# High parts of the weight slabs beside the retention: from GpSimd to ScalarE

## The chip, the cores and the metric

The kernel runs on one core of one Trainium2 chip. The metric is the device time of one execution in microseconds (us). The engines are named as in the profile: PE is TensorE (matmuls, and transposes done as matmuls; PEld is its weight load), DVE is VectorE, ACT is ScalarE, POOL is GpSimd, SP is SyncE, which here issues the DMAs.

## The reference

The program is one layer of a streaming encoder on a sequence of 1024 tokens with 1024 features, all in float32. The part that matters here is the retention branch and the input projection that runs beside it:

```python
h = rmsnorm(x, ln_pre_mix[layer])
p = h @ w_in[layer]                       # one combined projection
(g_q, g_k, g_v, g_r, g_lr, r_q, r_k, r_v, r_g, a_gla, a_ret) = jnp.split(p, split_at, axis=-1)
...                                       # gated linear attention (GLA) branch
rq = rope(r_q.reshape(b, s, RET_HEADS, RET_DK), positions)
rk = rope(r_k.reshape(b, s, RET_HEADS, RET_DK), positions)
# retention_mixer, per chunk and head:
scores = jnp.einsum('bhnd,bhmd->bhnm', qi, ki) * intra_decay
o = jnp.einsum('bhnm,bhme->bhne', scores, vi) + jnp.einsum('bhnd,bhde->bhne', qi * q_decay, state)
state = chunk_decay * state + jnp.einsum('bhmd,bhme->bhde', ki * k_decay, vi)
# then
o_ret = head_layernorm(o_ret) * silu(r_g)
y_ret = o_ret @ w_ret_out[layer]
merged = sigmoid(a_gla) * y_gla + sigmoid(a_ret) * y_ret
...                                       # m @ W_o, norm, and the ConvFFN
```

`rope` is the rotary embedding: the first half of a head's features becomes x1·cos − x2·sin, the second x1·sin + x2·cos.

## The kernel before

**Products in three parts.** Each large float32 product is made of three fast matmuls: both operands are split into a high part (the value written in TensorE's fp32r format) and a low part (the value minus its high part), and `product3` (lines 421 to 423) adds high·high, low·high and high·low. So each slab of weights, 128 partitions by 1024 columns, is needed as `w_hi` and `w_lo`, made from the loaded `w_raw`. All three have four slots (`RING`), used in turn.

**How slabs move.** SP loads slab n into `w_raw` (`stream_load`, line 1355) once slab n−4 has been split (`slab_ready`). Somebody writes `w_hi` (this counts `hi_split` up), then somebody writes `w_lo` (this counts `slab_ready` up), and PE waits for `slab_ready` before it uses the slab (`side_piece`, line 1320). `w_hi` may be overwritten once PE has used slab n−4 (`mm_half`). In other stages of this program ScalarE writes `w_hi` with a copy of the same shape and GpSimd writes `w_lo` (lines 3109 and 3098, the down projection of the FFN, for one). Beside the GLA and the retention, GpSimd does both, in `split_slab` (line 1360).

**The retention.** It has 32 steps (`RS`), e = 0 to 31: token tile e // 4 (128 tokens) and head e % 4. Every engine runs its own list of instructions in a fixed order, one list per function (`ret_pe`, `ret_dve`, `ret_act`, `ret_pool`, `ret_sp`), and they meet only at semaphores. What one step holds, in order:

- PE, step e: wait for the rotated queries and keys of step e (`r_rope`), transposes of the keys (line 2058), scores (2067), for e < 28 a quarter of a projection slab (`side_piece`, 12 matmuls), the transposes of the output of step e−2 (2107), the output of step e−1 (2085 and, from the second token tile on, 2088), the input to the state of step e−1 (2098).
- DVE, step e: weights of step e (1985), gate of step e−2 (1994), the mean and variance of the output of step e−1 (2003, 2005), its normalisation (2010), the state (2019 or 2021).
- ACT, step e: a scaled copy of the transposed keys of step e (`keys`, 1949), the reciprocal deviation of step e−1 (`rstd`, 1956 and 1959, which wait for DVE's 2005), in odd steps the eviction of a side bank (1341).
- POOL, step e: the rotation of step e (1920, 1921, 1929, 1931) and the decayed queries (1934). 1929 waits until PE has made the output of step e−4. For e = 0, 4, ..., 24 a slab follows (`split_slab`: 1365 for `w_hi`, 1368 for `w_lo`), and one more after step 31.
- SP, step e: stores, loads of the inputs of step e+4 and, for e = 0, 4, ..., 28, the load of a slab.

The slab that POOL splits in step e is used by PE from step e+8 on (the slabs split in the steps 20 and 24 and after the loop belong to the next stage).

Of the kernel before, what the change touches and what calls it, by code (L numbers as in the profile page):

```python
# [19 lines left out]
F32 = mybir.dt.float32  # L20
F32R = mybir.dt.float32r
I32 = mybir.dt.int32
ALU = mybir.AluOpType
ACT = mybir.ActivationFunctionType
# [71 lines left out]
SL_SIDE = SL_VAL + 4 * N_PLAIN + 1  # L96
# [14 lines left out]
BLOCK_LOADS = ROW_LOADS + BLOCK_GROUPS  # L111
RING = 4
# [90 lines left out]
def build(nc, x, positions, w_stream, w_dec, b_dec, ln_post_mix, ln_post_ffn, ln_cols_in, conv_in,  # L203
          ident_in, interval_in, masks_in, ret_dec_in, ret_q_in, ret_k_in, inv_freq_in, eps_in, out):
    ctx = ExitStack()
    with ctx:
        sem = {name: ctx.enter_context(nc.semaphore(name)) for name in SEMS}
# [15 lines left out]
        def sb(stack, name, shape, dt=F32):  # L223
            return stack.enter_context(nc.sbuf_tensor(name, list(shape), dt))
# [12 lines left out]
        w_raw = sb(ctx, "w_raw", (P, RING, D))  # L237
        w_hi = sb(ctx, "w_hi", (P, RING, D), F32R)
        w_lo = sb(ctx, "w_lo", (P, RING, D), F32R)
# [165 lines left out]
        raw_in = [sem[f"raw_in{j}"] for j in range(RING)]  # L405
# [902 lines left out]
        def tile_cols(t):  # L1308
            return slice(t * P, t * P + P)
# [26 lines left out]
        def side_evict(act, q):  # L1336

            act.wait_ge(sem["mm_half"], 2 * SL_SIDE + q + 1)
            if q >= SIDE_SLOTS:
                act.wait_ge(side_stored[q % SIDE_SLOTS], 16 * (q // SIDE_SLOTS))  # L1340
            nc.scalar.activation(side_out[:, q % SIDE_SLOTS, :], psum[:, SIDE_BANK + q % 2, :], ACT.Copy
                                 ).then_inc(sem["side_evac"], 1)
# [17 lines left out]
        def split_slab(pool, n):  # L1360

            j = n % RING
            pool.wait_ge(raw_in[j], 16 * (n // RING + 1 + BLOCK_LOADS))
            pool.wait_ge(sem["mm_half"], 2 * n - 2 * RING + 2)
            nc.gpsimd.tensor_tensor(w_hi[:, j, :], w_raw[:, j, :],
                                    zero_col[:, :].to_broadcast((P, D)), ALU.add).then_inc(sem["hi_split"], 1)
            pool.wait_ge(sem["hi_split"], n + 1)
            nc.gpsimd.tensor_tensor(w_lo[:, j, :], w_raw[:, j, :], w_hi[:, j, :].bitcast(F32),
                                    ALU.subtract).then_inc(sem["slab_ready"], 1)


        def gla_gates(sp, t):

            if t:
                sp.wait_ge(sem["g_og"], 2 * t)
            sp.dma_start(g_gate[:, :, :], proj_d[ROW_GR:ROW_GR + GLA_KT, :, tile_cols(t)]
                         .rearrange("r p n -> p r n")).then_inc(sem["g_gate_in"], 16)
# [14 lines left out]
        def gla_first_loads(sp):  # L1392

            sp.dma_start(masks[:, :], masks_in).then_inc(sem["g_tab_in"], 16)
            sp.dma_start(e_t[:, 0, :], interval_in).then_inc(sem["g_tab_in"], 16)
            gla_log_a_load(sp, 0)
            for t in range(2):
                gla_tile_loads(sp, t)
            gla_gates(sp, 0)
# [413 lines left out]
        def last_tile(e):  # L1813
            return e >= RS - HEADS
# [94 lines left out]
        def ret_pool(pool):  # L1909
            pool.wait_ge(sem["r_tab_in"], 64)  # L1910
            pool.wait_ge(sem["g_S"], 2 * NT * HEADS)
            for e in range(RS):
                t, h, b = e // HEADS, e % HEADS, e % 2
                x4 = r_x[:, h, 0:4, :]
                pool.wait_ge(r_in[h], 16 * t + 16)
                cos = cossin[:, 0, tile_cols(t)].unsqueeze(1).to_broadcast((P, 4, P))
                sin = cossin[:, 1, tile_cols(t)].unsqueeze(1).to_broadcast((P, 4, P))
                if e >= 2:
                    pool.wait_ge(sem["r_rope"], 2 * e - 2)
                nc.gpsimd.tensor_tensor(r_xcb[:, b, :, :], x4, cos, ALU.mult).then_inc(sem["r_xc"], 1)  # L1920
                nc.gpsimd.tensor_tensor(r_xsb[:, b, :, :], x4, sin, ALU.mult).then_inc(sem["r_xs"], 1)
                pool.wait_ge(sem["r_xc"], e + 1)
                pool.wait_ge(sem["r_xs"], e + 1)
                if t:
                    pool.wait_ge(sem["r_o"], e - 3)
                xc = r_xcb[:, b, :, :].rearrange("p (a c) n -> p a c n", c=2)
                xs = r_xsb[:, b, :, :].rearrange("p (a c) n -> p a c n", c=2)
                qk = r_qk[:, h, :, :].rearrange("p (a c) n -> p a c n", c=2)
                nc.gpsimd.tensor_tensor(qk[:, :, 0, :], xc[:, :, 0, :], xs[:, :, 1, :], ALU.subtract
                                        ).then_inc(sem["r_rope"], 1)  # L1930
                nc.gpsimd.tensor_tensor(qk[:, :, 1, :], xs[:, :, 0, :], xc[:, :, 1, :], ALU.add
                                        ).then_inc(sem["r_rope"], 1)
                pool.wait_ge(sem["r_rope"], 2 * e + 2)
                nc.gpsimd.tensor_tensor(r_qdb[:, h, :, :], r_qk[:, h, 0:2, :],
                                        ret_q[:, h, :].unsqueeze(1).to_broadcast((P, 2, P)),
                                        ALU.mult).then_inc(sem["r_qd"], 1)
                if e % 4 == 0 and e < RS - HEADS:
                    split_slab(pool, SL_SIDE + 19 + e // 4)
            split_slab(pool, SL_SIDE + 26)

        def ret_act(act):
            act.wait_ge(sem["r_tab_in"], 64)
            act.wait_ge(sem["g_og"], 2 * NT)

            def keys(e):
                act.wait_ge(sem["r_kT"], e + 1)
                if e >= 2:
                    act.wait_ge(sem["r_u"], e - 1)
                nc.scalar.activation(r_kdt[:, e % 2, :], psum[:, KT_BANK, 0:RET_DK], ACT.Copy,
                                     scale=ret_k[:, e % HEADS:e % HEADS + 1]).then_inc(sem["r_kd"], 1)  # L1950

            def rstd(e):

                b = e % 2
                act.wait_ge(sem["r_mv"], e + 1)
                nc.scalar.activation(r_rsb[:, b, 0:1], r_mvb[:, b, 1:2], ACT.Ln, bias=eps_col[:, 0:1]
                                     ).then_inc(sem["r_lnv"], 1)
                act.wait_ge(sem["r_lnv"], e + 1)
                nc.scalar.activation(r_rsb[:, b, 1:2], r_rsb[:, b, 0:1], ACT.Exp, scale=-0.5
                                     ).then_inc(sem["r_rstd"], 1)  # L1960

            for e in range(RS):
                if not last_tile(e):
                    keys(e)
                if e:
                    rstd(e - 1)
                if e < SIDE_STEPS and e % 2:
                    side_evict(act, 4 * NT + 2 + e // 2)
                if e >= MIXED_STEP:
                    for i in range(4 * (e - MIXED_STEP), 4 * (e - MIXED_STEP) + 4):  # L1970
                        mixed_hi(act, i)
            rstd(RS - 1)
            for i in range(8, 16):
                mixed_hi(act, i)
# [186 lines left out]
        def mixed_hi(act, i):  # L2161

            act.wait_ge(a_in[i % RING], 16 * (i // RING) + 32 + 16 * NT + 16)
            if i == 0:
                act.wait_ge(sem["mm_half"], 2 * SL_YGLA)
            if i == 16:
                act.wait_ge(sem["r_og"], RS)
                for b in range(2):
                    act.wait_ge(r_ogst[b], 8 * RS)
            if i == 16 + RET_KT:  # L2170
                act.wait_ge(sem["mm_half"], 2 * SL_YRET)
            nc.scalar.activation(mixed_parts(i)[0], a_raw[:, i % RING, :], ACT.Copy).then_inc(sem["a_hi"], 1)
# [1237 lines left out]
        @block.gpsimd  # L3410
        def _(pool):
            nc.gpsimd.memset(zero_col[:, :], 0.0).then_inc(sem["zero_set"], 1)
            nc.gpsimd.memset(eps_col[:, :], EPS).then_inc(sem["zero_set"], 1)
            pool.wait_ge(sem["zero_set"], 2)
            split_slabs(pool, 0, SL_LR)
            rows_pool(pool)
            split_slabs(pool, SL_LR + RING, SL_SIDE + 3, BLOCK_LOADS)
            gla_pool(pool)
            ret_pool(pool)
            split_slabs(pool, SL_YGLA + 3, SL_MIX, BLOCK_LOADS)  # L3420
            mix_pool(pool)
            up_pool(pool)
            slabs_lo(pool, SL_DOWN + RING, N_USED - SL_DOWN - RING)
# [55 lines left out]
```

## Time and profile before

| | us |
|---|---|
| median of 3 runs | 2281.41 (2281.05 to 2281.82) |
| the profiled execution, its own time | 2281.12 |
| its span, first to last instruction | 2279.3 |
| PE busy | 2243.6 (98%) |
| POOL busy | 1538.8 (68%) |
| DVE busy | 1209.4 (53%) |
| ACT busy | 669.2 (29%) |

The span is what the trace shows; the execution's own time is 1.8 us longer. "Busy" counts an engine's own instructions. A wait is idle time of an engine, put down to the instruction that released it. Matmuls are pipelined: a 512-column matmul is shown with 0.39 us, but the next one starts about 0.23 us after it.

### The profile page before, as it was taken

The numbers are of one execution on the slowest core, as the hardware profiler recorded it, in microseconds if no ns is written. First come the engines' busy times: TensorE is split into PE (matmuls) and PEld (weight loads), VectorE is DVE, ScalarE is ACT, GpSimd is POOL, SyncE is SP. The second block draws the span as 40 slices with busy tenths as digits, with TensorE's granted clock in tenths as the row PEclk, the third lists the DMA queues.
The fourth block names the chain that finished last, engine by engine and source line by source line (L and its number), as shares of the span: only waits on it lengthen the run. The fifth ranks groups of instructions, "written<-read, shape, count | busy, mean of one in ns | idle before, by whom it ended". The sixth has DMA issues, their size and how long they took to land. (4 is left out here: it accounts for less than half of the span.)

```text
span 2279.3 us, 27552 instructions
## 1 busy us (share of the span) xinstructions
PE 2243.6 (98%) x10462; PEld 1829.5 (80%) x10462; DVE 1209.4 (53%) x1271; ACT 669.2 (29%) x1029; POOL 1538.8 (68%) x946
## 2 busy tenths in 40 slices
PE   8999999999999999999999999999899999999998
PEld 7888888899888888876665888878778888888887
DVE  6322222222728877854446434323867777776564
ACT  4323333221222222211113211114444444443422
POOL 5787777766446555578664468870999999964442
PEclk9999999999999999999999999999999999999999
DMA  4333333322362333265557556642222222246444
GB/s 178 102 111 111 111 111 111 111 93 96 124 229 88 110 111 121 85 214 168 162 165 213 194 204 216 223 171 108 78 74 84 84 83 84 93 160 209 143 140 152
DMA packets 174716, 309.06 MB, mean 136 GB/s; under 512 B 12224, under 2 KB 90304, under 8 KB 174592
## 3 DMA queue, kind: packets, MB, share of 16 engines
q1 hardware_dynamic: 174160, 306.27, 40.8%
q8 instruction: 81, 1.33, 0.2%
q10 hardware_dynamic: 432, 1.11, 0.1%
q14 instruction: 43, 0.35, 0.0%
HBM read 217.16 MB, written 90.18 MB: 135 GB/s over the span
## 5 line engine op out<-in xcount | busy, mean ns | idle before, releaser
L421 PE MATMUL psum<-act_hi,w_hi 128*128 128x512 f32 x1272 | 505.4, 397 | 5.0 <-DVE act_lo L2178 1.4
L423 PE MATMUL psum<-act_hi,w_lo 128*128 128x512 f32 x1272 | 496.7, 391 | 0.0
L422 PE MATMUL psum<-act_lo,w_hi 128*128 128x512 f32 x1272 | 495.4, 389 | 0.0
L421 PEld LDWEIGHTS psum<-act_hi,w_hi 128*128 128x128 f32 x1272 | 239.0, 188 | 54.8 <-issue 2.9
L423 PEld LDWEIGHTS psum<-act_hi,w_lo 128*128 128x128 f32 x1272 | 238.7, 188 | 51.5
L422 PEld LDWEIGHTS psum<-act_lo,w_hi 128*128 128x128 f32 x1272 | 239.2, 188 | 46.9
L455 POOL TENSOR_TENSOR w_hi<-w_raw,zero_col 128x1024 fp32r<-128x1024 f32 x53 | 109.0, 2057 | 165.4 <-PE psum L423 147.7
L3098 POOL TENSOR_TENSOR w_lo<-w_raw,w_hi 128x1024 fp32r<-128x1024 f32 x44 | 110.5, 2515 | 126.5 <-ACT w_hi L3109 126.5
L1530 POOL TENSOR_TENSOR k_lev<-e_t,g_x 128x896 f32<-128x896 f32 x32 | 96.3, 3010 | 127.6 <-ACT e_t L1477 92.4
L1062 POOL TENSOR_TENSOR w_lo<-w_raw,w_hi 128x512 fp32r<-128x512 f32 x80 | 105.1, 1314 | 64.9 <-ACT w_hi L1020 64.9
L2796 DVE TENSOR_TENSOR d_lob<-d_raw,d_hib 128x512 fp32r<-128x512 f32 x44 | 101.9, 2320 | 86.9 <-ACT d_hib L2790 86.9
L458 POOL TENSOR_TENSOR w_lo<-w_raw,w_hi 128x1024 fp32r<-128x1024 f32 x53 | 143.8, 2714 | 4.2
L421 PE MATMUL psum<-w_hi,act_hi 128*128 128x512 f32 (+1 forms) x384 | 139.7, 364 | 1.8 <-POOL w_lo L458 1.5
L422 PE MATMUL psum<-w_lo,act_hi 128*128 128x512 f32 (+1 forms) x384 | 139.3, 363 | 0.0
L423 PE MATMUL psum<-w_hi,act_lo 128*128 128x512 f32 (+1 forms) x384 | 139.2, 363 | 0.0
L421 PE MATMUL psum<-w_hi,d_hib 128*128 128x512 f32 x352 | 137.3, 390 | 1.4 <-DVE act_f L2835 0.7
L422 PE MATMUL psum<-w_lo,d_hib 128*128 128x512 f32 x352 | 137.0, 389 | 0.0
L423 PE MATMUL psum<-w_hi,d_lob 128*128 128x512 f32 x352 | 137.0, 389 | 0.0
L3056 POOL TENSOR_TENSOR w_lo<-w_raw,w_hi 128x512 fp32r<-128x512 f32 x80 | 126.3, 1588 | 2.9 <-ACT w_hi L3138 2.8
L421 PE MATMUL psum<-a_sums,w_hi 128*128 128x512 f32 x320 | 124.5, 389 | 0.0
L422 PE MATMUL psum<-a_sums,w_hi 128*128 128x512 f32 x320 | 124.5, 389 | 0.0
L423 PE MATMUL psum<-a_sums,w_lo 128*128 128x512 f32 x320 | 124.5, 389 | 0.0
(300 smaller groups left out, 4947.3 us busy)
## 6 DMA issues: line engine op xcount, KB each, us to landing
w_raw<-in_w_stream SPq DMA_DIRECT2D x225, 512.0 KB, 4.0
proj_scratch<-stage SPq DMA_DIRECT2D x40, 512.0 KB, 5.0
r_x<-proj_scratch SPq DMA_DIRECT2D x64, 256.0 KB, 3.2
value_scratch<-stage SPq DMA_DIRECT2D x24, 512.0 KB, 3.6
proj_scratch<-side_out SPq DMA_DIRECT2D x48, 256.0 KB, 3.0
d_raw<-ffn_scratch SPq DMA_DIRECT2D x44, 256.0 KB, 3.7
ffn_scratch<-u_lin_v SPq DMA_DIRECT2D x20, 512.0 KB, 5.8
r_v<-value_scratch SPq DMA_DIRECT2D x32, 256.0 KB, 2.7
```

The costliest lines, as they stand in the source:

```text
L421: nc.tensor.matmul(o, s_hi, m_hi, start=start, stop=False)
L422: nc.tensor.matmul(o, s_hi, m_lo, start=False, stop=False)
L423: return nc.tensor.matmul(o, s_lo, m_hi, start=False, stop=stop)
L455: nc.gpsimd.tensor_tensor(w_hi[:, j, :], w_raw[:, j, :], zero_col[:, :].to_broadcast((P, D)), ALU.add).then_inc(sem["hi_split"], 1)
L458: nc.gpsimd.tensor_tensor(w_lo[:, j, :], w_raw[:, j, :], w_hi[:, j, :].bitcast(F32), ALU.subtract).then_inc(sem["slab_ready"], 1)
L1062: nc.gpsimd.tensor_tensor(w_lo8[:, n % 8, :], row_block(p, i), w_hi8[:, n % 8, :].bitcast(F32), ALU.subtract).then_inc(sem["u_lo"], 1)
L1530: nc.gpsimd.tensor_tensor(k_lev[:, b, :, :], levels, key.unsqueeze(1).to_broadcast((P, NL, P)), ALU.mult).then_inc(sem["g_klev"], 1)
L2796: nc.vector.tensor_tensor(d_lob[:, slot, :], d_raw[:, slot, :], d_hib[:, slot, :].bitcast(F32), ALU.subtract).then_inc(sem["d_lo"], 1)
L3056: nc.gpsimd.tensor_tensor(w_lo8[:, n % 8, :], block_raw(p, i), w_hi8[:, n % 8, :].bitcast(F32), ALU.subtract).then_inc(sem["u_lo"], 1)
L3098: nc.gpsimd.tensor_tensor(w_lo[:, j, :], w_raw[:, j, :], w_hi[:, j, :].bitcast(F32), ALU.subtract).then_inc(sem["slab_ready"], 1)
```

## The change

A slab beside the retention is no longer split by POOL alone. ScalarE writes the high part, at the end of its steps 0, 4, ..., 28 (`side_slab_hi`, with the two waits that POOL had: the slab has landed, and PE is through with slab n−4). GpSimd writes the low part at the old place (`side_slab_lo`, with the wait for `hi_split` only). `split_slab` stays as it was for the GLA stage.

```diff
+        def side_slab_hi(act, n):
+
+            j = n % RING
+            act.wait_ge(raw_in[j], 16 * (n // RING + 1 + BLOCK_LOADS))
+            act.wait_ge(sem["mm_half"], 2 * n - 2 * RING + 2)
+            nc.scalar.activation(w_hi[:, j, :], w_raw[:, j, :], ACT.Copy).then_inc(sem["hi_split"], 1)
+
+        def side_slab_lo(pool, n):
+
+            j = n % RING
             pool.wait_ge(sem["hi_split"], n + 1)
             nc.gpsimd.tensor_tensor(w_lo[:, j, :], w_raw[:, j, :], w_hi[:, j, :].bitcast(F32),
                                     ALU.subtract).then_inc(sem["slab_ready"], 1)
...
                 if e % 4 == 0 and e < RS - HEADS:
-                    split_slab(pool, SL_SIDE + 19 + e // 4)
-            split_slab(pool, SL_SIDE + 26)
+                    side_slab_lo(pool, SL_SIDE + 19 + e // 4)
+            side_slab_lo(pool, SL_SIDE + 26)
...
                 if e < SIDE_STEPS and e % 2:
                     side_evict(act, 4 * NT + 2 + e // 2)
+                if e % 4 == 0:
+                    side_slab_hi(act, SL_SIDE + 19 + e // 4)
                 if e >= MIXED_STEP:
```

GpSimd's list at the end of step 4, before (the first row is the last of step 4, the two slab rows follow, then step 5 begins):

```order
L1934 TENSOR_TENSOR r_qdb<-r_qk,ret_q 128x256 [waits r_rope]
L1365 TENSOR_TENSOR w_hi<-w_raw,zero_col 128x1024 [waits mm_half,raw_in1]
L1368 TENSOR_TENSOR w_lo<-w_raw,w_hi 128x1024 [waits hi_split]
L1920 TENSOR_TENSOR r_xcb<-r_x,cossin 128x512 [waits r_rope,r_in1]
L1921 TENSOR_TENSOR r_xsb<-r_x,cossin 128x512
L1929 TENSOR_TENSOR r_qk<-r_xcb,r_xsb 128x2x128 [waits r_o,r_xs,r_xc]
```

The same place after the change (its lines are numbered 15 higher):

```order
L1949 TENSOR_TENSOR r_qdb<-r_qk,ret_q 128x256 [waits r_rope]
L1383 TENSOR_TENSOR w_lo<-w_raw,w_hi 128x1024 [waits hi_split]
L1935 TENSOR_TENSOR r_xcb<-r_x,cossin 128x512 [waits r_rope,r_in1]
L1936 TENSOR_TENSOR r_xsb<-r_x,cossin 128x512
L1944 TENSOR_TENSOR r_qk<-r_xcb,r_xsb 128x2x128 [waits r_o,r_xs,r_xc]
```

One instruction of POOL is gone, and the wait for `hi_split`, which POOL's own instruction just ahead used to satisfy, is now for ScalarE. The rotation of step 5 stands behind it.

ScalarE's list around step 4, before (the eviction that ends step 3; of step 4 the copy of the keys and the two instructions of the reciprocal deviation; the copy of the keys of step 5):

```order
L1341 ACTIVATE side_out<-psum 128x512 [waits side_st2,mm_half]
L1949 ACTIVATE r_kdt<-psum,ret_k 128x256 [waits r_u,r_kT]
L1956 ACTIVATE r_rsb<-r_mvb,eps_col 128x1 [waits r_mv]
L1959 ACTIVATE r_rsb<-r_rsb 128x1 [waits r_lnv]
L1949 ACTIVATE r_kdt<-psum,ret_k 128x256 [waits r_u,r_kT]
```

And after:

```order
L1341 ACTIVATE side_out<-psum 128x512 [waits side_st2,mm_half]
L1964 ACTIVATE r_kdt<-psum,ret_k 128x256 [waits r_u,r_kT]
L1971 ACTIVATE r_rsb<-r_mvb,eps_col 128x1 [waits r_mv]
L1974 ACTIVATE r_rsb<-r_rsb 128x1 [waits r_lnv]
L1377 ACTIVATE w_hi<-w_raw 128x1024 [waits mm_half,raw_in1]
L1964 ACTIVATE r_kdt<-psum,ret_k 128x256 [waits r_u,r_kT]
```

The copy stands behind the reciprocal deviation of step 3, whose first instruction waits for DVE's statistics. In step 0 there is no such instruction, and the copy stands behind the keys alone. The lists of PE, DVE and SP hold the same instructions in the same order as before.

## Rows read from the trace of the kernel before

**Rows 1.** The page's busy times by engine.
```profile
PE 2243.6 (98%) x10462; PEld 1829.5 (80%) x10462; DVE 1209.4 (53%) x1271; ACT 669.2 (29%) x1029; POOL 1538.8 (68%) x946
```
**Rows 2.** Stretch of the retention: us, busy (count) by engine, PE clock, DMA, GB/s.
```profile
1000.00:1233.00 233.00, 231.43 (x912) 146.30 (x911) 110.52 (x208) 36.17 (x106) 176.63 (x171) 1.00 0.57 168
```
**Rows 3.** Waits in 985:1245: who waited for whom, total us, times, longest.
```profile
POOL r_qk L1929 <- PE psum L2088: 50.3, 17, 3.4
...
PE psum L2107 <- DVE r_ogb L1994: 2.1, 1, 2.1
...
PE psum L2058 <- POOL r_qk L1931: 1.0, 1, 1.0
...
PE psum L2085 <- POOL r_qdb L1934: 0.3, 1, 0.3
```
**Rows 4.** PE in time, first rows of steps 6 and 8: start us, us, instruction.
```profile
1037.20 0.38 PE L2058 MATMUL psum<-ident,r_qk 128*128 128x128 f32 x2
...
1053.54 0.38 PE L2058 MATMUL psum<-ident,r_qk 128*128 128x128 f32 x2
```
**Rows 5.** ACT in time at the end of step 5; DVE and ACT in step 6.
```profile
1036.64 0.29 ACT L1956 ACTIVATE r_rsb<-r_mvb,eps_col 128x1 f32<-128x1 f32 x1 [6.70 <-DVE r_mvb L2005]
...
1037.07 0.58 ACT L1341 ACTIVATE side_out<-psum 128x512 f32<-128x512 f32 x1
...
1043.85 0.70 DVE L2003 BATCH_NORM_STATS2 r_bst<-psum 128x6 f32<-128x512 f32 x1 [1.83 <-PE psum L2088]
...
1044.80 0.29 ACT L1956 ACTIVATE r_rsb<-r_mvb,eps_col 128x1 f32<-128x1 f32 x1 [6.71 <-DVE r_mvb L2005]
```
**Rows 6.** POOL in time: the slab of step 8, then step 9.
```profile
1042.53 1.89 POOL L1365 TENSOR_TENSOR w_hi<-w_raw,zero_col 128x1024 fp32r<-128x1024 f32 x1
1044.50 2.37 POOL L1368 TENSOR_TENSOR w_lo<-w_raw,w_hi 128x1024 fp32r<-128x1024 f32 x1
1046.83 1.29 POOL L1920 TENSOR_TENSOR r_xcb<-r_x,cossin 128x512 f32<-128x512 f32 x1
...
1050.18 0.72 POOL L1931 TENSOR_TENSOR r_qk<-r_xsb,r_xcb 128x256 f32<-128x256 f32 x1
```
**Rows 7.** A handover from ACT to POOL in the down projection, in time.
```profile
2157.75 1.06 ACT L3109 ACTIVATE w_hi<-w_raw 128x1024 fp32r<-128x1024 f32 x1 [1.38 <-PE psum L423]
...
2158.89 2.40 POOL L3098 TENSOR_TENSOR w_lo<-w_raw,w_hi 128x1024 fp32r<-128x1024 f32 x1 [0.55 <-ACT w_hi L3109]
2164.32 3.43 POOL L3098 TENSOR_TENSOR w_lo<-w_raw,w_hi 128x1024 fp32r<-128x1024 f32 x1 [3.04 <-ACT w_hi L3109]
```
**Rows 8.** ACT, POOL and PE in time, steps 0 and 1.
```profile
999.80 0.47 ACT L1949 ACTIVATE r_kdt<-psum,ret_k 128x256 f32<-128x256 f32 x1
...
997.19 2.38 POOL L1368 TENSOR_TENSOR w_lo<-w_raw,w_hi 128x1024 fp32r<-128x1024 f32 x1
...
1002.89 0.72 POOL L1931 TENSOR_TENSOR r_qk<-r_xsb,r_xcb 128x256 f32<-128x256 f32 x1
...
1003.67 0.44 PE L2058 MATMUL psum<-ident,r_qk 128*128 128x128 f32 x2 [0.96 <-POOL r_qk L1931]
```
**Rows 9.** End of the program: PE's last matmul, then stretches of Rows 2's kind.
```profile
2272.02 0.39 PE L423 MATMUL psum<-w_hi,d_lob 128*128 128x512 f32 x1
...
2274.00:2274.50 0.50, 0.00 (x0) 0.00 (x0) 0.47 (x2) 0.00 (x0) 0.00 (x0) 1.00 0.00 0
2274.50:2275.00 0.50, 0.00 (x0) 0.00 (x0) 0.47 (x2) 0.00 (x0) 0.00 (x0) 0.56 0.00 0
2275.00:2276.00 1.00, 0.00 (x0) 0.00 (x0) 1.00 (x2) 0.00 (x0) 0.00 (x0) 0.50 0.00 0
```
**Rows 10.** PE in time: first transposes of the program; four transposes in the retention.
```profile
4.79 2.39 PE L540 MATMUL psum<-ident 128*128 128x128 f32 x10 [4.79 <-DMA ident<-in_ident_in]
7.09 2.46 PE L551 MATMUL psum<-ident,x_tok 128*128 128x128 f32 x16
...
1040.64 0.60 PE L2107 MATMUL psum<-ident,r_onb 128*128 128x128 f32 x4
```

More of the change, by code:

```diff
@@ L1369, in split_slab @@
                                     ALU.subtract).then_inc(sem["slab_ready"], 1)
+        def side_slab_hi(act, n):
[5 more added lines that the diff above has]
+            j = n % RING
+            pool.wait_ge(sem["hi_split"], n + 1)
+            nc.gpsimd.tensor_tensor(w_lo[:, j, :], w_raw[:, j, :], w_hi[:, j, :].bitcast(F32),
+                                    ALU.subtract).then_inc(sem["slab_ready"], 1)
         def gla_gates(sp, t):
```

## The prediction

> **What bounds the kernel now.** I read the page's busy times first: PE is busy for 98% of the span, POOL for 68%, ACT for 29% [rows 1]. So time is won or lost only where PE stands still, and the change touches one stage. The view of that stretch says the same of it: in 233 us of the retention PE is busy 231.4, POOL 176.6, ACT 36.2, and the granted clock is 1.00 throughout [rows 2]. Then the waits of the stage: POOL waits for PE, 50.3 us in 17 waits (the rotation of step e needs the output of step e−4), and PE waits for POOL twice, 1.0 and 0.3 us [rows 3]. POOL is ahead of PE there, not behind. By how much: POOL has finished the rotation of step 8 and begins to split a slab at 1042.53 [rows 6], and PE begins step 8 at 1053.54 [rows 4], 11 us later. The slab work of POOL lies in that lead and costs PE nothing.
>
> A step from 5 on lasts 8.17 us on PE: from 1037.20 to 1053.54 it does two, 6 and 7 [rows 4]. I call the start of step e on PE T(e).
>
> **What the change removes.** Eight GpSimd instructions of 1.89 us [rows 6], 15.1 us of POOL. At PE they are worth nothing, as POOL's lead covers them; at most the two short waits go, 1.3 us [rows 3].
>
> **What it adds: a wait that ties POOL to PE.** POOL's low part in step e now waits for ScalarE's copy, which stands in ACT's list behind the reciprocal deviation of step e−1. That waits for DVE's statistics, and these for PE's output matmuls of step e−1, which PE does late in its own step e [rows 5]. So POOL can't pass the slab of step e before PE is nearly through with step e. And behind the low part, in POOL's list, stands the rotation of step e+1, for which PE waits before anything of step e+1. The lead is lost every fourth step, whatever it was. In terms of T(e), from step 6, the chain is:
>
> - the reciprocal deviation starts at T+7.60 (1044.80 less 1037.20) [rows 4, 5];
> - the next instruction of ACT starts 0.43 later (1036.64 to 1037.07) [rows 5]: the copy, at T+8.03;
> - POOL's low part starts 1.14 after the start of such a copy, of 1.06 us (2157.75 to 2158.89) [rows 7]: T+9.17;
> - the rotation of the next step starts 2.33 after it (1044.50 to 1046.83) and ends 4.07 later (1046.83 to 1050.18, plus 0.72) [rows 6]: T+15.57;
> - PE starts 0.06 after that (1002.89 plus 0.72 is 1003.61, PE at 1003.67) [rows 8]: T+15.63.
>
> PE would have begun step e+1 at T+8.17. It stands idle for 7.46 us. Step 4 is shorter, as the output of step 3 has no product with the state, but has the same gap: the output comes as much earlier as the next step.
>
> How often: the waits after steps 4, 8, 12, 16, 20 and 24 block a rotation: six times 7.46 are **44.8 us**. The slab of step 28 is split after POOL's loop, and the one copy of 1.06 us on ACT lies in its idle time: nothing. Between two gaps POOL needs 4.6 us a step (176.6 us less eight slabs of 4.26, over 31 steps [rows 2, 6]), PE 8.17, so the steps e+2 to e+4 are not late, and the rotation of e+4 is ready in time; each gap is then paid in full, and none is paid twice.
>
> In step 0 there is no reciprocal deviation. The keys are copied at 999.80 for 0.47 us; the copy of the slab starts some 0.04 before that ends, at 1000.23, the low part at 1001.37 in place of 997.19 [rows 8]. POOL is late by 4.18 us, and PE waits for it there already (0.96 us), so all of it counts: **4.2 us**.
>
> **The lists behind the waits.** SP's load of a slab in step e waits for the low part, until about T+11.5 in place of T+8.2, where the wait for PE's state matmuls leaves it anyway. Behind it are loads that are needed three and four steps on: nothing. ACT has nothing to do after the copy until PE begins step e+1. DVE finishes step e in the gap. The slabs are used eight steps later: no new wait at `slab_ready`.
>
> The low part might be slower at its new time. In the down projection it takes 2.40 us once and 3.43 us the next time, with DVE at work on two SBUF tiles beside it [rows 7]. In the retention the old low part took 2.37 us [rows 6]; DVE's work just after T+9.2 is the state update with one input from PSUM, which ran beside the old ones too. I take 2.33 and keep six times 1.0 us above it as a bound. The Trainium skill ("GPSIMD Engine Reference", Specifications) says that POOL shares its SBUF interfaces with VectorE, with contention when DVE has "two SBUF inputs"; by that rule the state update does not slow it, which is the value that I take.
>
> **What the gaps do to the clock.** At the end of the program PE's last matmul ends at 2272.41, the granted clock is 1.00 until 2274.5 and 0.50 from about 2274.56 on [rows 9]: 2.15 us after PE went quiet it is at the lower level, 1.2 GHz. Gaps of 7.46 us, and the one of 5.1 us in step 0 (0.96 plus 4.18), are longer than that, so PE should come back from all seven at the lower level. What the way back costs shows at the start of the program: 10 and 16 transposes take from 4.79 to 9.55, 4.76 us. In the retention four such take 0.60 us of 0.27 each, one every 0.11 us [rows 10]; 26 of them would take 25 times 0.11 plus 0.27, 3.02 us. The clock column reads 1.00 there, but the transposes say that the first of them ran more slowly, and that this cost 1.74 us. Seven times 1.74 are **12.2 us**. Bounds: 0, as after the pause of 2.1 us that PE has in the retention [rows 3], and twice the price, 24.4 us, as the start is one case only.
>
> The Trainium skill speaks against this change here ("TensorE: Matmul & The Clock Gate", Part 1): "the default state is throttled, and activity releases the throttle." By that rule the gaps cost more than their idle time, and the trace's end and start agree. Without it the sum would be the idle time alone, the second rival.
>
> **The sum.** 44.8 + 4.2 + 12.2 = 61.2 us. The profiled execution took 2281.12 us, so 2342.3. The median of the runs is 0.3 above that execution, which is less than anything here: I forecast 2342.
>
> **The rivals.**
> 1. *Gaps as forecast, the clock does not matter much* (it stays up in most gaps, or comes back at once): 2281.1 + 49.0 = 2330.1. For it: the stage itself shows no drop [rows 2]. Against it: rows 9 and 10. Chance 0.13. The mirror image, each return costing twice as much: 2354.5, chance 0.08.
> 2. *The wait is hidden*: ScalarE's copy would be early enough that POOL keeps its lead. Then nothing changes: 2281. For it: ACT is idle for most of the stage [rows 2]. Against it: ACT's idle time is spent in the list ahead of the copy, waiting for DVE (6.7 us at a time [rows 5]), so the copy can't be early. Chance 0.02.
> 3. *The other side*: POOL's relief is what counts. Where PE waits for POOL's rotation (1.0 us before step 1, and 0.3 us for the queries of step 30 [rows 3]), an instruction of 1.89 us less would end both waits: 2281.1 − 1.3 = 2279.8. It decides from the point at which the copy ends before POOL is at the low part, that is at T−11 or so in place of T+9.1. Rows 5 exclude this for all steps but 0, and for step 0 the copy ends at 1001.3, 6 us after POOL got there. A mistake in my reading of the lists would be needed. Chance 0.01.
>
> **How the numbers follow.** The forecast has 0.76. Its own spread is that of the clock's price (a return may take somewhat less or more than the one case), and of the gap: 0.1 us in a handover is 0.6 us, and a low part slowed by DVE up to 6 us. The range from 2332 to 2353 takes in all but the ends of rival 1 and leaves out the quick cases. What a measurement here can tell from no change is about 0.2%, 4.6 us. Slower by more than that: 0.97; within it: 0.02; faster: 0.01.
>
> **What the profile of the changed kernel would show.** PE waits for POOL's rotation before the steps 5, 9, 13, 17, 21 and 25, each 7.4 to 7.5 us, and 5.1 us before step 1. POOL's low part waits for ACT's copy seven times, and the wait of POOL for PE's output (50.3 us now) shrinks to little. ACT's copies are 1.06 us each. The granted clock of the stage is below 1.00, with a stretch of 0.50 in each gap and in the first microseconds after it, where matmuls of 512 columns come twice as slowly. Stages before and after the retention keep their times. Wrong would be the forecast if PE's gaps are short or missing (then POOL does not stand behind ScalarE as the lists say), or if the clock stays at 1.00 (rival 1), or if a gap is longer than 7.5 us, so that another handover in the chain costs more than its row.

## The result, and the profile after

The changed kernel takes 2346.68 us, median of 4 runs (2345.66 to 2347.62), against 2281.23 of before (4 runs, 2280.49 to 2281.82). The ratio is 1.028, 95% interval 1.0267 to 1.0293: 65.5 us slower. The forecast was 2342, range 2332 to 2353.

The page's busy times of the kernel after, and its stretch 1000 to 1233 (columns as in [rows 2]), answer to [rows 1, 2]:

```profile
PE 2262.0 (96%) x10462; PEld 1843.5 (79%) x10462; DVE 1213.2 (52%) x1271; ACT 677.6 (29%) x1037; POOL 1521.8 (65%) x938
```
```profile
1000.00:1233.00 233.00, 191.93 (x717) 124.85 (x716) 83.44 (x155) 33.21 (x86) 124.70 (x126) 0.90 0.44 129
```

ACT has eight instructions more, POOL eight fewer and 17.0 us less work. PE, which was busy for 231.4 of these 233 us, is now busy for 191.9, and its mean granted clock is 0.90. (In 233 us the longer kernel gets through fewer steps, so less work of each engine falls into the stretch.) PE's busy time over the whole span is 18.4 us *longer* with the same matmuls, so some of them ran slowly.

The waits of the stage (985 to 1320) in the kernel after, which answer to [rows 3]:

```profile
ACT r_rsb L1971 <- DVE r_mvb L2022: 202.8, 32, 9.3
POOL w_lo L1383 <- ACT w_hi L1377: 121.6, 8, 21.3
...
PE psum L2075 <- POOL r_qk L1946: 48.3, 7, 7.2
...
POOL r_qk L1944 <- PE psum L2105: 4.3, 2, 3.4
```

They are turned round. POOL used to wait 50.3 us for PE's outputs, and PE 1.0 us for the rotation. Now PE waits 48.3 us for the rotation, in seven waits, and POOL waits 121.6 us for ScalarE's copy. A long wait of POOL is only its old lead, now spent in front of the copy; what costs is the row in which PE waits.

The chain at step 8, instruction by instruction, answers to [rows 4 to 6]. PE begins the step:

```profile
1069.97 0.38 PE L2075 MATMUL psum<-ident,r_qk 128*128 128x128 f32 x2
...
1074.70 1.88 PE L2105 MATMUL psum<-r_st,r_qdb 128*128 128x512 f32 x4
1076.42 1.88 PE L2115 MATMUL psum<-r_v,r_kdt 128*128 128x512 f32 x4
1085.50 0.69 PE L2075 MATMUL psum<-ident,r_qk 128*128 128x128 f32 x2 [7.21 <-POOL r_qk L1946]
```

DVE's statistics, then ScalarE's reciprocal deviation and the copy:

```profile
1076.62 0.70 DVE L2020 BATCH_NORM_STATS2 r_bst<-psum 128x6 f32<-128x512 f32 x1 [1.83 <-PE psum L2105]
```
```profile
1077.57 0.30 ACT L1971 ACTIVATE r_rsb<-r_mvb,eps_col 128x1 f32<-128x1 f32 x1 [6.71 <-DVE r_mvb L2022]
...
1078.01 1.04 ACT L1377 ACTIVATE w_hi<-w_raw 128x1024 fp32r<-128x1024 f32 x1
```

POOL's low part and the rotation of step 9 behind it:

```profile
1079.12 2.35 POOL L1383 TENSOR_TENSOR w_lo<-w_raw,w_hi 128x1024 fp32r<-128x1024 f32 x1 [20.46 <-ACT w_hi L1377]
1081.43 1.26 POOL L1935 TENSOR_TENSOR r_xcb<-r_x,cossin 128x512 f32<-128x512 f32 x1
...
1084.72 0.72 POOL L1946 TENSOR_TENSOR r_qk<-r_xsb,r_xcb 128x256 f32<-128x256 f32 x1
```

From the start of the step these are 7.60, 8.04, 9.15, 11.46 and 15.47 us, and PE goes on at 15.53. The forecast had 7.60, 8.03, 9.17, 11.50, 15.57 and 15.63.

The clock in this gap, in the kernel after (columns as in [rows 2]):

```profile
1078.30:1081.90 3.60, 0.00 (x0) 0.00 (x0) 1.84 (x3) 0.75 (x1) 2.78 (x2) 1.00 0.34 93
1082.00:1085.40 3.40, 0.00 (x0) 0.00 (x0) 0.00 (x0) 0.00 (x0) 3.27 (x4) 0.50 0.58 169
1085.50:1088.70 3.20, 3.20 (x11) 2.81 (x12) 0.29 (x1) 0.47 (x1) 3.17 (x3) 0.50 0.19 57
1088.90:1092.00 3.10, 3.10 (x15) 2.27 (x14) 0.69 (x1) 0.00 (x0) 3.02 (x4) 1.00 0.02 5
```

PE is quiet from 1078.30. The granted clock falls to 0.50 (1.2 GHz) at 1081.98, while PE stands still; PE goes on at 1085.50, and 3.30 us pass before the clock is back. About half of that is lost, 1.56 us.

**Where the 66.5 us are** (the two profiled executions, 2347.62 and 2281.12). I compared the start of the scores in all 32 steps of the two traces. The delay grows in only two places of each group of four steps e to e+3 (e = 0, 4, ..., 24): before step e+1 (the gap), and within it (the clock).

| step | scores before, us | scores after, us | delay | gap | cost of the clock |
|---|---|---|---|---|---|
| 0 | 999.33 | 999.67 | 0.34 | | |
| 1 | 1003.95 | 1008.54 | 4.59 | 3.98 | 2.69 |
| 5 | 1029.26 | 1043.90 | 14.64 | 7.36 | 2.06 |
| 9 | 1061.92 | 1085.99 | 24.07 | 7.37 | 1.56 |
| 13 | 1094.59 | 1127.58 | 32.99 | 7.36 | 2.85 |
| 17 | 1127.25 | 1170.47 | 43.22 | 7.38 | 1.94 |
| 21 | 1159.92 | 1212.44 | 52.52 | 7.36 | 1.46 |
| 25 | 1192.59 | 1253.92 | 61.33 | 7.36 | 2.83 |
| 31 | 1230.03 | 1293.92 | 63.89 | | |
| sum | | | | 48.2 | 15.4 |

(Of the growth up to such a step 0.27 us is counted as clock, since the transposes ahead of the scores take 0.48 in place of 0.21 us.) The rest is 0.3 us before step 0, 2.4 us after the retention and 0.2 us outside the span: 0.3 + 48.2 + 15.4 + 2.4 + 0.2 = 66.5.

The gaps' 48.2 us and the 48.3 us of PE's waits above agree by chance. The wait before step 1 holds 1.0 us that PE waited before the change too, and each of the others is shown 0.16 us shorter than PE's delay (7.20 for 7.36), as a matmul's shown end lies that far behind the start of the next.

The seven prices differ, but in each the clock cost 0.47 of the time that it took to come back: 5.65, 4.43, 3.31, 6.08, 4.16, 3.14 and 6.03 us, in the order of the table.

The 2.4 us after the retention are a wait for loaded tiles that comes out longer (2.0 us in one piece; the longest such wait of before was 1.1), and once more the clock. Kernel after, PE in time, then the stretch's clock:

```profile
1312.06 0.40 PE L423 MATMUL psum<-act_hi,w_lo 128*128 128x512 f32 x1
1314.46 0.80 PE L421 MATMUL psum<-act_hi,w_hi 128*128 128x512 f32 x1 [2.00 <-DVE act_lo L2195]
```
```profile
1314.00:1315.00 1.00, 0.54 (x1) 0.50 (x2) 1.00 (x3) 0.94 (x2) 0.00 (x0) 0.54 1.05 339
```

This place varies from kernel to kernel, whatever was changed: over the eight traces beside before's, the span less the delay at step 31 lies between 0.6 us under and 2.6 us over the span of before. I don't count it as an effect of the change, though no run isolates it.

### The profile page after: what moved, and what is told of

The parts are those of the page before. It is cut to its first block and busy times, and to the rows that moved or that the text cites. A ratio compares the mean times of both kernels' runs of the same rounds, so it can differ in the third digit from the quotient of the medians.

```text
span 2345.6 us, 27552 instructions
## 1 busy us (share of the span) xinstructions
PE 2262.0 (96%) x10462; PEld 1843.5 (79%) x10462; DVE 1213.2 (52%) x1271; ACT 677.6 (29%) x1037; POOL 1521.8 (65%) x938
## 3 DMA queue, kind: packets, MB, share of 16 engines
q10 hardware_dynamic: 432, 1.11, 0.1%
## 5 line engine op out<-in xcount | busy, mean ns | idle before, releaser
L421 PE MATMUL psum<-act_hi,w_hi 128*128 128x512 f32 x1272 | 511.2, 402 | 6.2 <-DVE act_lo L2195 2.6
```

Source lines behind the costliest of these rows:

```text
L421: nc.tensor.matmul(o, s_hi, m_hi, start=start, stop=False)
```

## The experiments

All are set against the kernel before, run beside them on the same chip. The first four share a median of 2282.48 us for it, the last three 2281.93. Where a time is compared with its expectation, the ratio is the better measure, as the expectations start from 2281.2.

### The copy four steps earlier

```diff
-                if e % 4 == 0:
-                    side_slab_hi(act, SL_SIDE + 19 + e // 4)
+                if (e + 4) % 4 == 0 and e + 4 < RS:
+                    side_slab_hi(act, SL_SIDE + 19 + (e + 4) // 4)
...
             rstd(NT - 1, 0)
+            side_slab_hi(act, SL_SIDE + 19)
             side_evict(act, 4 * NT)
```

(Here and in the one-step version `side_slab_hi` also waits for `hi_split` to reach n, so that the slabs are counted in order.)

> The changed kernel, with ScalarE's copy of a slab four steps earlier in its list (the first one in the tail of the GLA work). Theory (POOL's rotation of step e+1 stands behind a low part that waits for a late copy): the copy is done long before POOL gets to the low part, POOL has its lead again, PE's seven waits for the rotation (48.3 us) and the drops of the clock vanish: 2280 to 2281.5 us, within 0.1% of before, with about 1 us to win before step 1. Rival (the copy itself disturbs, by ScalarE's work or by two engines at one slab): the time stays near 2347, or at least some 10 us above 2281.

Measured: 2281.42 us (11 runs), ratio 0.9995 (0.9986 to 1.0004). PE's seven waits for the rotation are gone, the clock is 1.00 in the whole stage, step 0 is 1.2 us shorter than before's and every other step the same. Eight copies on ScalarE and eight low parts alone on GpSimd cost nothing; the copies' place in ScalarE's list cost 65 us.

### The copy in the middle of the step

```diff
                     keys(e)
+                if e % 4 == 0:
+                    side_slab_hi(act, SL_SIDE + 19 + e // 4)
                 if e:
                     rstd(e - 1)
                 if e < SIDE_STEPS and e % 2:
                     side_evict(act, 4 * NT + 2 + e // 2)
-                if e % 4 == 0:
-                    side_slab_hi(act, SL_SIDE + 19 + e // 4)
```

> The changed kernel, with the copy in the same steps but ahead of the reciprocal deviation instead of behind it, right after the copy of the keys. Theory (the wait for DVE's statistics ahead of the copy is what makes it late): the low part starts about 2.1 us after the start of PE's step e in place of 9.2, the rotation of step e+1 is ready about 8.5 us after it: gaps of 0.3 us in the steps from 8 on, some 2 us at step 4 (whose step is 6.44 us long), and step 0 as in the changed kernel (4.0 us and 2.7 us by the clock): 2281.2 + 6.7 + 2 + 1.5 = about 2291, up to 2294 if the clock falls at step 4 too. Rival (any hand-over between the engines costs the gap, wherever the copy stands in the step): 2347.

Measured: 2291.48 us (5 runs), ratio 1.0039 (1.0026 to 1.0052), 8.9 us. In its trace the steps are late by 3.97 us at step 1 (and 1.41 by the clock), 1.95 at step 5 and 0.24 at each of the steps 9 to 25, close to the 4.0, 2 and 0.3 that were expected; of the clock 2.7 had been expected. ACT at step 8 of this kernel:

```profile
1061.52 0.47 ACT L1964 ACTIVATE r_kdt<-psum,ret_k 128x256 f32<-128x256 f32 x1
1061.90 1.05 ACT L1377 ACTIVATE w_hi<-w_raw 128x1024 fp32r<-128x1024 f32 x1
1068.71 0.29 ACT L1971 ACTIVATE r_rsb<-r_mvb,eps_col 128x1 f32<-128x1 f32 x1 [5.76 <-DVE r_mvb L2022]
```

The copy runs in what used to be ACT's idle time, 5.8 us ahead of the statistics. Moving it past two instructions takes back 57 of 65 us, so the wait in front of it is the cause. The delay of 1.95 us at step 5, in which PE stood still for 1.73, did not bring the clock down.

### Work for PE in the gaps

```diff
                 if e and not last_tile(e - 1):
                     state_inputs(e - 1)
+                if e % 4 == 0 and e < RS - HEADS:
+                    pe.wait_ge(sem["r_P"], e + 1)
+                    for _ in range(60 if e else 40):
+                        nc.tensor.transpose(psum[:, RS_BANK, P:2 * P], ident[:, :], ident[:, :])
```

> The changed kernel, with work for PE in the gaps: after its step e (e = 0, 4, ..., 24) 60 transposes of the identity into an unused part of a PSUM bank (40 in step 0), about 6.4 us (4.3) at the full clock, which is less than the gaps of 7.4 (5.1) us. They compute nothing that is used. Theory (15.4 us of the loss are matmuls at the lower clock after the gaps): the gaps stay, the clock stays at 1.00, and the time falls to 2281.2 + 48.2 = 2329.5, up to 2332. Rival (the slower matmuls after the gaps come from something else, or the 15 us are waits): no change, 2347, or more.

Measured: 2332.55 us (4 runs), ratio 1.0222 (1.0207 to 1.0238), which from 2281.2 gives 2331.9, the upper end of what was expected. Against 1.028 that is 13 us less, by *adding* 400 transposes. Its stage, and the gap before step 9 on PE:

```profile
1000.00:1283.00 283.00, 277.57 (x1320) 190.82 (x1320) 112.02 (x209) 44.37 (x115) 166.11 (x165) 1.00 0.47 139
```
```profile
1073.47 6.71 PE L2146 MATMUL psum<-ident 128*128 128x128 f32 x60
1080.88 0.44 PE L2075 MATMUL psum<-ident,r_qk 128*128 128x128 f32 x2 [0.69 <-POOL r_qk L1946]
```

The steps 5, 9, ..., 25 still come 7.46 us late each, step 1 is 4.07 late, and nothing is lost within a step: 48.8 us in the stage in place of 63.6. So nearly all of the 15.4 us within the steps was the clock, 14.8 us by this comparison (the delay before each step is 0.1 us longer than in the table), and the gaps are waits that a faster clock of PE does not shorten. Transposes alone, 60 in 6.71 us, kept the clock at 1.00.

### The low part one step later, the copy as late as ever

```diff
-                if e % 4 == 0 and e < RS - HEADS:
+                if e % 4 == 1 and e < RS - HEADS:
                     side_slab_lo(pool, SL_SIDE + 19 + e // 4)
```

> The changed kernel, ScalarE's list untouched; GpSimd makes the low part of a slab one step later, behind the rotation of step e+1 instead of ahead of it. Theory (the loss is the rotation that stands behind the low part): the low part starts 1.0 us after PE has begun step e+1, the rotation of step e+2 is ready 7.4 us after it, before the 8.17 us of the step are over: no gaps, 2280 to 2282, although every copy is as late as in the changed kernel. SP's load of a slab waits a step longer; nothing needs it soon. Rival (the late copy costs by itself, or through SP's queue behind the load of the slab): 2300 or more.

Measured: 2280.65 us (11 runs), ratio 0.9991 (0.9982 to 1.0000). POOL in step 9 of this kernel; PE began step 9 at 1060.65:

```profile
1061.64 2.41 POOL L1383 TENSOR_TENSOR w_lo<-w_raw,w_hi 128x1024 fp32r<-128x1024 f32 x1 [10.96 <-ACT w_hi L1377]
...
1067.33 0.73 POOL L1946 TENSOR_TENSOR r_qk<-r_xsb,r_xcb 128x256 f32<-128x256 f32 x1
```

The low part starts 0.99 us into the step and still waits 11 us for a copy that comes as late as in the changed kernel, and the rotation of step 10 is ready 7.4 us into a step of 8.17. PE waits for nothing. This separates the late copy, which by itself costs nothing, from the rotation that stands behind it, through which the whole loss comes. Since SP's load of the slab waits a step longer too and nothing is lost, SP's queue is not the cause either.

### The copy one step earlier

```diff
-                if e % 4 == 0:
-                    side_slab_hi(act, SL_SIDE + 19 + e // 4)
+                if (e + 1) % 4 == 0 and e + 1 < RS:
+                    side_slab_hi(act, SL_SIDE + 19 + (e + 1) // 4)
```

> The changed kernel with the copy only one step earlier in ScalarE's list (end of step e-1 for the slab of step e; the one of step 0 in the tail of the GLA work). Theory (the chain from PE's output matmuls over the statistics and the copy to the rotation, 7.4 us longer than the step allows): moved by one step of 8.17 us the chain ends 0.8 us before PE needs the rotation, so no gap from step 8 on; at step 4, which is preceded and followed by steps of 6.44 us, a gap of 1.0 us stays, too short for the clock to fall: 1.0 us more than with the copy four steps early, 2281 to 2283. Rival (POOL needs its whole lead back, a copy just in time still costs): 2290 or more.

Measured: 2281.75 us (11 runs), ratio 0.9999 (0.9990 to 1.0008). No gap from step 8 on, as expected, and one before step 5, but of 1.53 us and not 1.0. PE's row in this kernel, and ACT's at the end of step 3:

```profile
1028.92 0.44 PE L2077 MATMUL psum<-ident,r_qk 128*128 128x128 f32 x2 [1.31 <-POOL r_qk L1948]
```
```profile
1020.87 0.58 ACT L1341 ACTIVATE side_out<-psum 128x512 f32<-128x512 f32 x1
1021.35 1.05 ACT L1378 ACTIVATE w_hi<-w_raw 128x1024 fp32r<-128x1024 f32 x1
```

I had forgotten that the steps 3, 7, ... are odd and end with an eviction: the copy stands 0.48 us further back. That is the missing half microsecond. (The 1.53 us are the delay of the scores of step 5; the row shows 1.31 idle, as a wait is shown some 0.2 us shorter than the delay.)

### One slab only

```diff
-                if e % 4 == 0:
+                if e == 8:
                     side_slab_hi(act, SL_SIDE + 19 + e // 4)
...
-                    side_slab_lo(pool, SL_SIDE + 19 + e // 4)
-            side_slab_lo(pool, SL_SIDE + 26)
+                    (side_slab_lo if e == 8 else split_slab)(pool, SL_SIDE + 19 + e // 4)
+            split_slab(pool, SL_SIDE + 26)
```

> The kernel before, with the change for one slab of eight, that of step 8: ScalarE copies it at the end of step 8, GpSimd makes its low part; all others as before. Theory (each gap is paid in full and on its own): one wait of PE of 7.4 us before step 9 and a return of the clock that costs 1.5 to 2.9 us: 2281.2 + 8.9 to 10.3 = 2290 to 2291.5, a seventh of the whole loss. Rival (POOL's lead of 11 us takes up a single late copy, and the loss comes from seven of them in a row): 2281 to 2283.

Measured: 2291.28 us (4 runs), ratio 1.0044 (1.0028 to 1.0059), about 10 us with an interval of 6.4 to 13.5. The trace is sharper: the scores of step 9 come 7.62 us too late against those of step 8, and step 10 adds 1.25; in the terms of the table a gap of 7.35 and 1.5 for the clock, together 8.8. POOL's lead of 11 us takes up nothing, even once, since what POOL waits for here hangs on an output that PE makes late in that same step.

### The low part made twice

```diff
             nc.gpsimd.tensor_tensor(w_lo[:, j, :], w_raw[:, j, :], w_hi[:, j, :].bitcast(F32),
+                                    ALU.subtract).then_inc(sem["g_tab"], 1)
+            pool.wait_ge(sem["g_tab"], n - SL_SIDE - 17)
+            nc.gpsimd.tensor_tensor(w_lo[:, j, :], w_raw[:, j, :], w_hi[:, j, :].bitcast(F32),
                                     ALU.subtract).then_inc(sem["slab_ready"], 1)
```

> The changed kernel with the low part of the eight slabs made twice by GpSimd, one after the other. Theory (POOL's work behind the late copy lies on the path of PE): each of the seven gaps grows by 2.4 us, 16.7 us together, to 2363.4, give or take 3 us for the clock. Rival (POOL has time to spare, as its 65% busy says, and the copy's lateness alone sets the gap): 2347 to 2350.

Measured: 2361.5 us (4 runs), ratio 1.0344 (1.0328 to 1.0360). From 1.028 that is 14.6 us more; 16.7 was expected. POOL and PE's waits in this kernel:

```profile
1085.10 2.35 POOL L1383 TENSOR_TENSOR w_lo<-w_raw,w_hi 128x1024 fp32r<-128x1024 f32 x1 [21.04 <-ACT w_hi L1377]
1087.52 2.34 POOL L1386 TENSOR_TENSOR w_lo<-w_raw,w_hi 128x1024 fp32r<-128x1024 f32 x1
```
```profile
PE psum L2078 <- POOL r_qk L1949: 65.2, 7, 9.6
```

The second low part takes its 2.42 us in each of seven gaps: PE's waits grow from 48.3 to 65.2 us, 16.9. So POOL's work behind the copy is on PE's path one for one, in a stage in which POOL is idle for nearly half of the time. In the stage the whole delay grows from 63.6 to 81.0 us, 17.4. The ratios give 2.8 us less than that. In the two traces the part after the stage is 2.6 us shorter, a place where the kernels vary anyway.

## Why the prediction was right, point by point

- **POOL is ahead, and its relief is worth nothing.** Right. POOL did 17.0 us less, 15.1 of them the eight copies, and nothing got faster; with the copy out of the way the gain is the one wait of 1.0 us before step 1 [rows 3] and some 0.2 us beside it. The other wait, of 0.3 us for the queries of step 30, stayed.
- **The chain of the gap, 7.46 us.** Right to 0.1 us: 7.36. Its parts came from rows of four places; the copy to the low part took 1.11 (1.14 taken), the low part 2.31 (2.33), the rotation 4.01 (4.07).
- **Six full gaps, one of 4.2 us, none at step 28.** Right: 44.2 and 3.98 us (44.8 and 4.2 forecast). One working figure was off: the stretch of [rows 2] holds seven slabs of POOL and not eight, so POOL needs 4.7 us a step and not 4.6, still far below 8.17.
- **The low part is not slowed by DVE.** Right: 2.35 us beside DVE's state update, where another stage had shown 3.43 [rows 7]. The Trainium skill ("GPSIMD Engine Reference", Specifications) names contention with DVE instructions in a two-port mode or with two SBUF inputs; the state update has one of its inputs in PSUM, and the 2.35 us agree. What [rows 7] don't show is what DVE did there. The same DVE instruction, with two SBUF tiles as inputs, ran beside both low parts:

```profile
2158.99 3.38 DVE L2843 SCALAR_TENSOR_TENSOR act_f<-act_f,stat,d_ln 128x1024 f32<-128x1024 f32 x1
...
2164.22 1.29 DVE L2843 SCALAR_TENSOR_TENSOR act_f<-act_f,stat,d_ln 128x1024 f32<-128x1024 f32 x1
```

  The first time POOL had begun 0.10 us earlier and kept its 2.40 us, and DVE took 3.38; the second time DVE had begun 0.10 us earlier and kept its 1.29, and POOL took 3.43. So in these two cases the one that began later paid, and a low part can be slowed or can slow DVE.
- **Nothing behind the waits of SP, ACT and DVE.** Right, as far as the stage goes: all steps that have no gap and no slow clock keep their length, from step 5 on 8.17 us.
- **The clock falls in all seven gaps.** Right. Its price was the mis-sized term: 12.2 us forecast from one case of 1.74, 15.4 measured, 1.46 to 2.85 each. The run with the transposes in the gaps gives 14.8 for the clock. The one case came from the quick end of the spread. At the start of the program a transpose is shown with 0.42 us, as it is at 0.50 after a gap, and this lasts some 3.3 us, from 4.79 until about 8.1; the seven returns took 3.14 to 6.08. It also holds short waits, some 0.2 of the 1.74 us. So the reading of [rows 10] as a slow clock was right, and to take one case for seven was what made the term too small.

```profile
L540 PE MATMUL psum<-ident x10: 421/421/473, 4.8 to 6.8; 128*128 128x128 f32 x10
```

  (Duration in ns, shortest, median and longest; at 1.00 it is 272.) The rule of the Trainium skill that I had weighed ("TensorE: Matmul & The Clock Gate", Part 1: without activity the clock is throttled) holds in all seven, where the clock is down 4.80 us after PE's last matmul at the latest. Where the prediction calls the idle time alone "the second rival", its first is meant.
- **Outside the retention nothing changes.** Off by 2.4 us in the profiled execution, a longer wait for loads and a drop of the clock in it. The scatter of the other kernels there is as large.

Against the forecast sum of 61.2 us the measured profile has 66.5: 0.8 less in the gaps, 3.2 more by the clock, 2.9 outside.

## What to carry to other kernels

Work that is moved to an idle engine is free only if its place in that engine's list comes before the consumer asks for it: an engine that is "29% busy" may spend its idle time in waits that stand ahead of the new instruction. Before such a move, follow what stands *ahead* of the new instruction back to the bottleneck engine, and what stands *behind* the new wait forward to it; if both ends are the bottleneck engine, a ring is closed and the lead is lost, here one of 11 us. Then either end can be moved. On GpSimd, the low part behind the next step's rotation took back all of the loss; on ScalarE, the copy one step earlier or more did, and the copy past two instructions took back 57 of 65 us. The second loss, the clock, came back when TensorE had something to do in the gaps.

## What the runs showed of the hardware

The granted clock is less regular than I had assumed. Over the seven gaps of the changed kernel it fell between 2.99 and 4.80 us after PE's last matmul, and 2.15 us after it at the end of the program before [rows 9]. At 1314.09 it fell 1.64 us into a pause of 2.00 us, which came soon after one of 0.57 us. The pause of 1.73 us in the version with the copy in mid-step left it at 1.00.

A pause of the same length need not end the same way. Near the end of the retention PE pauses for 2.06 us in all nine kernels, and the clock stays at 1.00 behind it in seven of them. In the version with the transposes in the gaps PE goes on at 1287.32, and the clock falls 1.37 us later, with PE at work; in the one with the low part twice it falls 0.64 us after the pause:

```profile
1287.32 0.63 PE L2124 MATMUL psum<-ident,r_onb 128*128 128x128 f32 x4 [2.06 <-DVE r_ogb L2011]
```
```profile
1287.40:1288.60 1.20, 1.20 (x8) 1.06 (x9) 1.20 (x3) 1.20 (x3) 0.00 (x0) 1.00 0.73 246
1288.70:1292.10 3.40, 3.40 (x9) 2.65 (x8) 2.77 (x6) 1.68 (x5) 0.00 (x0) 0.50 0.98 275
```

In the changed kernel the clock came back between 3.14 and 6.08 us after PE had gone on, at the costs of the table, 1.5 to 2.9 us, and in the version with the copy in mid-step after 2.88 us, for 1.4. At the start of the program the column reads 1.00 while the transposes run slowly [rows 10], so there the durations have to be read and not the column. What sets the place within this spread no run here settles.

None of the versions is a clear gain on the kernel before. The best, with the low part a step later, has the ratio 0.9991 with an interval that ends at 1.0000, and 1.2 us in step 0 is all that its trace gains within the retention.
